# Broadcasting modulation rows and preparing the attention context inside the expert rounds of a one-core fp32 two-block transformer

## The reference, cut to what matters

```python
def second_block(x, c, ctx, c_ctx, w_mod, b_mod, norm_mix, ...):
    for i in range(2):                                  # i = 0: attention, i = 1: Fourier mixing
        sh1, sc1, g1, sh2, sc2, g2 = split(silu(c) @ w_mod[i] + b_mod[i], 6)
        h = rms_norm(x, norm_mix[i]) * (1 + sc1) + sh1
        if i == 0:
            csh1, csc1, *_ = split(silu(c_ctx) @ w_mod[i] + b_mod[i], 6)
            h_c = rms_norm(ctx, norm_mix[i]) * (1 + csc1) + csh1       # 256 context tokens
            y = gqa_attention(h, h_c, ...)              # keys and values of h and of h_c, queries of h
        else:
            y = fft2(h) @ w_o
        x = x + g1 * y
        x = x + g2 * hier_moe(rms_norm(x, norm_ffn[i]) * (1 + sc2) + sh2, ...)
    return rms_norm(x, final_norm)
```

## Time and profile before

| what | value |
|---|---|
| median of 3 runs | 2091.72 us |
| the profiled execution's own time | 2091.08 us |
| its span, first to last instruction | 2089.4 us |
| TensorE matmul busy | 1580.1 us (76%) |
| VectorE, ScalarE, GpSimd busy | 424.2, 258.0, 94.3 us |
| moved by DMA | 710.85 MB, 340 GB/s over the span |
| mean granted TensorE clock | 0.89 of 2.4 GHz |
| chain that ended last | DMA 47%, PE 40%, DVE 7%, ACT 2% |

### The profile page before, as it was taken

One profiled execution on the slowest core, in us unless ns is written; L12 is line 12 of the kernel. 1 busy time (PEld: TensorE's weight loads), 2 busy tenths in 40 slices (PEclk: granted clock), 3 DMA queues, 4 the chain that ended last, 5 costly groups with the idle time before them and its releaser, 6 DMA issues.

```text
span 2089.4 us, 22424 instructions
## 1 busy us (share of the span) xinstructions
PE 1580.1 (76%) x9852; PEld 730.5 (35%) x9852; DVE 424.2 (20%) x872; ACT 258.0 (12%) x539; POOL 94.3 (5%) x138
## 2 busy tenths in 40 slices
PE   8678877699878676899886766676687866676674
PEld 5445443384445343445432222222143322122221
DVE  0432111216431012365320000000034000000001
ACT  0220000025310001236100000000021000000000
POOL 1100000201100000020100000000000000000000
PEclk9799998799989999899998888888898988888887
DMA  9254999929959999059759999999944899999994
GB/s 376 70 221 203 423 424 423 360 97 385 370 191 423 423 424 414 19 202 372 298 218 424 424 423 423 423 424 424 422 182 186 351 423 423 423 424 424 423 424 203
DMA packets 122827, 710.85 MB, mean 340 GB/s; under 512 B 8408, under 2 KB 13448, under 8 KB 48992
## 3 DMA queue, kind: packets, MB, share of 16 engines
q1 hardware_dynamic: 116352, 697.14, 81.5%
q0 software_dynamic: 4272, 9.58, 1.5%
q10 hardware_dynamic: 2096, 2.57, 0.3%
HBM read 707.97 MB, written 1.05 MB: 339 GB/s over the span
## 4 chain that ended last, share of the span: by engine, by line
DMA 47%; PE 40%; DVE 7%; ACT 2%; SPq 1%; issue 1%; POOL 1%; ACTq 1%; DVEq 0%; POOLq 0%; PEldq 0%
DMA ring<-in_moe_w 22%; DMA work<-in_moe_w 10%; DMA ring<-in_moe_w_down 6%; DMA ring<-in_moe_w_up 5%; PE acc L1133 5%; PE pb L637 4%; PE pa L652 4%; DMA mod<-in_moe_w 3%; PE pb L624 3%; PE pa L670 2%; PE acc L917 2%; PE acc L711 2%; PE acc L1055 1%; PE acc L1900 1%; PE acc L1044 1%; SPq L580 1%
## 5 line engine op out<-in xcount | busy, mean ns | idle before, releaser
L637 PE MATMUL pb<-ring,XT 128*32 128x512 f32 x1440 | 275.1, 708 | 90.2 <-DMA ring<-in_moe_w 75.9
L652 PE MATMUL pa<-ring,work 128*32 128x512 f32 x928 | 195.2, 766 | 66.9 <-DMA ring<-in_moe_w 34.5
L637 PEld LDWEIGHTS pb<-ring,XT 128*32 128x32 f32 x1440 | 62.0, 125 | 247.4 <-DMA ring<-in_moe_w 115.5
L745 DVE TENSOR_TENSOR work<-work,pb 128x256 f32<-128x256 f32 (+1 forms) x32 | 17.7, 554 | 600.7 <-PE pb L637 456.7
L670 PE MATMUL pa<-work,HM 128*128 128x128 f32 x1024 | 130.3, 290 | 11.1 <-DVE work L733 11.1
L670 PEld LDWEIGHTS pa<-work,HM 128*128 128x128 f32 x1024 | 129.4, 206 | 24.9 <-issue 13.4
L711 PE MATMUL acc<-XT,work 128*128 128x512 f32 x256 | 118.4, 605 | 25.5 <-DVE XT L749 25.5
L637 PE MATMUL pb<-work,XT 128*32 128x512 f32 x448 | 102.4, 730 | 35.1 <-DMA work<-in_moe_w 35.1
L624 PE MATMUL pb<-ring,XT 128*32 128x256 f32 x1472 | 108.2, 391 | 26.4 <-DMA ring<-in_moe_w_up 17.4
L652 PE MATMUL pa<-work 128*32 128x512 f32 x448 | 90.2, 776 | 44.4 <-DMA work<-in_moe_w 27.1
L1133 PE MATMUL acc<-ring,XT 128*128 128x512 f32 x256 | 110.9, 594 | 2.7 <-ACT XT L1085 1.4
(11 more groups left out here) (392 smaller groups left out, 1706.9 us busy)
## 6 DMA issues: line engine op xcount, KB each, us to landing
ring<-in_moe_w SPq DMA_DIRECT2D x128, 2048.0 KB
work<-in_moe_w SPq DMA_DIRECT2D x44, 2048.0 KB
ring<-in_moe_w_up SPq DMA_DIRECT2D x24, 2048.0 KB
ring<-in_w_mod SPq DMA_DIRECT2D x48, 1024.0 KB
ring<-in_moe_w_gate SPq DMA_DIRECT2D x22, 2048.0 KB
ring<-in_moe_w_down SPq DMA_DIRECT2D x20, 2048.0 KB
mod<-in_moe_w SPq DMA_DIRECT2D x20, 2048.0 KB
work<-in_moe_w_down SPq DMA_DIRECT2D x12, 2048.0 KB
```

The lines of the kernel that those rows point to most:

```text
L637: last = nc.tensor.matmul(hbank[m][j * CAP:(j + 1) * CAP, :], m_xg[:, k, j * CAP:(j + 1) * CAP], slot_of(s0 + j // 2)[:, at:at + fn], star ...
L652: last = nc.tensor.matmul(pa[j * CAP:(j + 1) * CAP, h, :], m_ht[:, c, j * CAP:(j + 1) * CAP], slot_of(i)[:, at:at + 512], start=(c == 0), ...
```

## The change

The phases mod 0 and mod 1 are kept in the list but issue nothing. Their work is spread over the expert rounds:

- `rows_tensor` issues two row blocks in a round, after the gathered tokens are copied and ahead of the gate projection, into the two banks of `pa`; the stationary operand is one column of `select`, read with stride 0 over 128 columns. `rows_scalar` copies both blocks ahead of the silu. Rounds with row blocks: all 8 of moe 1 (first the context's four, then the token's twelve), rounds 1 to 5 of moe 2, and round 0 of moe 3 (the last two row blocks of layer 1, whose place is in use until the end of moe 2).
- `mod[:, 0:4096]` must be free of weights for that: `RETIRED` takes the three lent slots out of the ring in moe 1 after their first use (nine blocks, then a ring of six), and the one in `mod` in moe 2 (nine blocks, then a ring of eight).
- The context is loaded when round 0 of moe 1 has freed its six blocks. Its squares are taken in round 2, it is normed in round 3, multiplied and shifted by VectorE in rounds 4 and 5, and turned by TensorE in rounds 6 and 7, between the gate and the up projection (8 transposes into `pa`, copied by ScalarE).
- In gqa the keys and values of the context come first, as soon as moe 1 has ended on TensorE, and are copied by ScalarE; the squares of a token tile are taken as soon as its layer norm is done. The four row copies that stood ahead of them are gone.
- In fourier the squares start as soon as a tile is gated; the scale is made in round 3 of moe 2.

```diff
+RETIRED = {1: (6, 7, 8), 2: (8,)}
+MOD_ROWS = {1: {0: (12, 13), 1: (14, 15), **{g: (2 * g - 4, 2 * g - 3) for g in range(2, 8)}},
+            2: {g: (2 * g - 2, 2 * g - 1) for g in range(1, 6)}, 3: {0: (10, 11)}}
...
+        rest = [i for i in order if i not in RETIRED.get(ph.moe, ())] if ph.kind == "moe" else order
         for n in range(ph.slots()):
-            i = order[n % len(order)]
+            i = order[n] if n < len(order) else rest[(n - len(order)) % len(rest)]
...
                     last.then_inc(free[0], 2 * free[1])
+                    if m == 0:
+                        context_tensor(pe, ph, g)
...
             pe.wait_ge(r["xg_copied"], 2 * (t + 1) + START)
             if whole:
-                whole_up_tensor(pe, ph, wait_full, free, slot_of, hbank)
+                rows_tensor(pe, ph, g)
+                whole_up_tensor(pe, ph, g, wait_full, free, slot_of, hbank)
...
             pe.wait_ge(r["ht_copied"], t + 1 + START)
             if whole:
+                rows_done(pe, ph, g)
+                context_done(pe, ph, g)
                 whole_down_tensor(pe, ph, wait_full, free, slot_of)
...
             nc.scalar.copy(m_xg[:, 0:4, :], pa[:, 0, :].rearrange("p (k c) -> p k c", c=P)).then_inc(r["xg_copied"], 1)
+            if r is R[0]:
+                rows_scalar(act, ph, g)
             freed_gate(act)
             nc.scalar.activation(m_silu[:, 0:fn], pb[:, 0, 0:fn], ACT.Silu).then_inc(r["silu_done"], 1)
+            if r is R[0]:
+                context_scalar(act, ph, g)
...
+        def rows_tensor(pe, ph, g):
+            blocks = MOD_ROWS.get(ph.moe, {}).get(g, ())
...
             for i, n in enumerate(blocks):
-                if i == 0 or i == N_SHIFT_SCALE:
-                    pe.wait_ge(sel_ready, 2 * ph.layer + 1 + (i > 0))
-                if i >= 4:
-                    pe.wait_ge(row_copied, ph.rows0 + i - 3)
-                nc.tensor.matmul(mod_bank(i), d_sel[:, n, :], mod_rows[:, :], start=True, stop=True).then_inc(row_ps, 1)
-            pe.wait_ge(row_copied, ph.rows0 + len(blocks))
+                nc.tensor.matmul(pa[:, i, :], bc(select[:, n:n + 1], [P, P]), mod_rows[:, :], start=True, stop=True).then_inc(row_ps, 1)
...
+        def context_tensor(pe, ph, g):
+            if ph.moe == 1 and g >= ROUNDS - TT:
+                t = g - (ROUNDS - TT)
+                pe.wait_ge(cx_ready, 1)
+                rows_done(pe, ph, g)
+                for k in range(KC):
+                    last = nc.tensor.transpose(by_chunk(pa)[:, k, :], g_cx[:, t, k * P:(k + 1) * P], ident[:, :])
+                last.then_inc(cx_ps, 1)
...
         def gqa_tensor(pe, ph):
-            transpose_tensor(pe, HM, ph)
-            pe.wait_ge(xt_ready, 2 * (ph.xt + 1))
+            pe.wait_ge(R[0]["y_copied"], 2 * ROUNDS * 2 + START)
             for k in range(KC):
                 if k % 2 == 0:
                     slot_wait(pe, ph.slot0 + k // 2)
                 for t in range(TT):
+                    last = nc.tensor.matmul(pa[:, t, :], g_hct[:, k, t * P:(t + 1) * P], w_of(k)[:, D:D + 512],
+                                            start=(k == 0), stop=(k == KC - 1))
+            last.then_inc(kv_done, 1)
+            pe.wait_ge(cx_kv, 2 * TT)
+            transpose_tensor(pe, HM, ph)
+            pe.wait_ge(xt_ready, 2 * (ph.xt + 1))
+            for k in range(KC):
+                for t in range(TT):
                     last = nc.tensor.matmul(acc[:, 0, t * 512:(t + 1) * 512], XT[:, k, t * P:(t + 1) * P], w_of(k)[:, D:D + 512],
...
-            pe.wait_ge(cx_ready, 1)
-            transpose_tensor(pe, g_cx)
-            pe.wait_ge(xt_ready, 2 * (ph.xt + 2))
-            for k in range(KC):
-                for t in range(TT):
-                    last = nc.tensor.matmul(pa[:, t, :], g_hct[:, k, t * P:(t + 1) * P], w_of(k)[:, D:D + 512],
-                                            start=(k == 0), stop=(k == KC - 1))
-            last.then_inc(kv_done, 1)
...
         def gqa_scalar(act, ph):
+            for t in range(TT):
+                act.wait_ge(h_ready, TT * moe.lnh + t + 1)
+                square_scalar(act, X[:, t, :], 32 + t, flat_xt, tile_squares)
+            act.wait_ge(kv_done, 1)
+            for t in range(TT):
+                nc.scalar.copy(g_k[:, 2 + t, :, 0, :], pa[:, t, 0:256].rearrange("p (j e) -> p j e", j=NKV)).then_inc(cx_kv, 1)
+                nc.scalar.copy(g_v[:, 2 + t, :], pa[:, t, 256:512]).then_inc(cx_kv, 1)
             transpose_scalar(act, ph.xt, XT)
-            transpose_scalar(act, ph.xt + 1, g_hct)
...
         def ahead_pool(pool, ph):
             if plan[ph.i + 1].layer == 0:
-                pool.wait_ge(phase_done, ph.i)
-                pool.dma_start(ctx_in, a["ctx_2"][0].rearrange("(t p) d -> p t d", p=P)).then_inc(cx_loaded, 16)
+                pool.wait_ge(freed, ph.slot0 + 6)
+                pool.dma_start(g_cx, a["ctx_2"][0].rearrange("(t p) d -> p t d", p=P)).then_inc(cx_loaded, 16)
...
         def fourier_scalar(act, ph):
+            squares_scalar(act, ph.x0 - TT, flat_xt)
```

More of the change, by code:

```diff
@@ L79, in run_parts, with rows_before @@
     return [(w, 2 * pair, half), (w, 2 * pair + 1, half)]
+RETIRED = {1: (6, 7, 8), 2: (8,)}
+MOD_ROWS = {1: {0: (12, 13), 1: (14, 15), **{g: (2 * g - 4, 2 * g - 3) for g in range(2, 8)}},
+            2: {g: (2 * g - 2, 2 * g - 1) for g in range(1, 6)}, 3: {0: (10, 11)}}
+ROWS_BY = {"gqa": 16, "fourier": 26}
+def rows_before(moe, g):
+    return sum(len(ns) for m in MOD_ROWS for h, ns in MOD_ROWS[m].items() if (m, h) < (moe, g))
 class Place:
@@ new lines, in rows_tensor @@
+        def rows_tensor(pe, ph, g):
+            blocks = MOD_ROWS.get(ph.moe, {}).get(g, ())
+            if blocks:
+                layer = int(ph.moe > 1)
+                pe.wait_ge(bias_loaded, 16 * (layer + 1))
+                for n in (MODC - 2, MODC - 1):
+                    pe.wait_ge(rows_moved[n % 2], rows_count(layer, n))
+            for i, n in enumerate(blocks):
+                nc.tensor.matmul(pa[:, i, :], bc(select[:, n:n + 1], [P, P]), mod_rows[:, :], start=True, stop=True).then_inc(row_ps, 1)
@@ new lines, in rows_done, with rows_scalar @@
+        def rows_done(pe, ph, g):
+            if g in MOD_ROWS.get(ph.moe, {}):
+                pe.wait_ge(row_copied, rows_before(ph.moe, g) + 2)
+        def rows_scalar(act, ph, g):
+            blocks = MOD_ROWS.get(ph.moe, {}).get(g, ())
+            if (ph.moe, g) == (1, 2):
+                act.wait_ge(freed, ph.slot0 + 7)
+            if (ph.moe, g) == (1, 6):
+                act.wait_ge(cx_ready, 1)
+            if (ph.moe, g) == (2, 1):
+                act.wait_ge(freed, ph.slot0 + DEEP)
+            for i, n in enumerate(blocks):
+                act.wait_ge(row_ps, rows_before(ph.moe, g) + i + 1)
+                dst = mod[:, n * 512:(n + 1) * 512] if n < MODC else c_mod[:, (n - MODC) * 512:(n - MODC + 1) * 512]
+                nc.scalar.copy(dst, pa[:, i, :]).then_inc(row_copied, 1)
+            if (ph.moe, g) == (1, 2):
@@ L986, in weights_of, with context_scalar @@
+        def context_scalar(act, ph, g):
+            if ph.moe == 1 and g >= ROUNDS - TT:
+                t = g - (ROUNDS - TT)
+                act.wait_ge(cx_ps, t + 1)
+                nc.scalar.copy(g_hct[:, :, t * P:(t + 1) * P], by_chunk(pa)).then_inc(cx_copied, 1)
         def weights_of(w, cols, kk, i):
@@ L2156, in _ @@
                     router_vector(dve, ph, link)
-                    moe_other(dve, ph, lambda r, t, g, gate, up, every: round_vector(dve, ph, r, t, g, up, every), last=True)
-                    if ph.i + 1 < len(plan) and plan[ph.i + 1].kind == "mod":
-                        dve.sem_inc(work_free, 1)
+                    moe_other(dve, ph, lambda r, t, g, gate, up, every: round_vector(dve, ph, link, r, t, g, up, every), last=True)
                     if ph.fn == FN1:
@@ L2180, in make_plan @@
     slot = 0
-    moe = xt = h = ln = small = att = out_ = masked = rows = mix = x = 0
+    moe = xt = h = ln = small = att = out_ = masked = mix = x = 0
     for i, (kind, layer, fn) in enumerate(kinds):
@@ L2191, in make_plan @@
         ph.slot_mod = slot + {"nsa": 6, "gqa": 4}.get(kind, 0)
-        ph.rows0 = rows
-        rows += {0: 16, 1: 12}[layer] if kind == "mod" else 0
         ph.nout = {"ab": 5, "nsa": 8, "gqa": 8, "fourier": 2}.get(kind, 0)
```

143 lines of the change are left out of this document (71 added, 72 removed).

## The result

The changed kernel takes **2066.67 us** (median of 4 runs, 2064.21 to 2068.10), where the kernel before took 2091.17 in the same series (4 runs, 2090.08 to 2091.93): a ratio of 0.9882, 95% interval 0.9865 to 0.9899, 24.5 us less. Its profiled execution took 2068.10 us with a span of 2066.3.

A forecast was written before the change was run, and what follows sets the result against it. It took HBM to bound the expert phases and the engines' dependency chain the gaps between. Terms of -22.5, -3.3 and +1.8 summed to -24.0 us, giving a median of 2067.7 us, range 2061 to 2076.

The forecast's parts named there:

- Step 1: Moe 1 ends 5.4 us later, as block 13 waits for round 1's gate behind two rounds of rows; ends 4.3 to 8.8.
- Step 2: Layer norm to the tokens' keys: L1223 starts 5.4 us earlier, with the context's keys made beside the norm.
- the third rival: After moe 1, the context's keys are late (blocks late or TensorE cold), ending at 850: up to 5 us, 2072; chance 0.07.
- one of the two signs: Wrong if moe 1 ended over 10 us later, or TensorE still made the context's keys when the modulated tile was ready.
- Step 3: Behind L1223, the context's transposes, copy and L1232 leave the chain ahead of the keys' chain: -17.1 us.
- nothing is paid: L1223 stays warm between transposes (-2.1 us) and the DFT matmuls stay warm too (-2): 2063; chance 0.07.
- Step 4: Fourier stage after moe 2: input ready 5.3 us sooner, 2.0 lost to TensorE's clock after a pause: -3.3 us.
- Step 5: Moe 3, round 0: two row blocks ahead of the gate delay the first refill: +1.8 us, to 3.4.
- a starved ring: Moe 1, rounds 2 to 7: six slots starve DMA; at 5 us a round, 2097; chance 0.03.
- The worse start of moe 1: Row matmuls at 3.4 us, block 18 late, context displacing more: +10 to 12 instead of 5.4, 2073; chance 0.10.

The follow-up runs named there:

- no_load: The changed kernel with the context filled by a GpSimd memset instead of its 1 MiB load: 2067.59 us.
- ring_only: The kernel before with only the smaller rings (six slots in moe 1, eight in moe 2, after the first nine blocks): 2093.54 us.
- lent_no_load: The changed kernel with moe 1's own six slots taking blocks 0 to 5 and the context filled by GpSimd instead of loaded: 2066.48 us.
- own_first: The changed kernel with the context's key and value matmuls behind the tokens' own, as the kernel before had them: 2081.65 us.
- filler runs: Extra matmuls ahead of the Fourier stage: nine in the changed kernel, 2064.22 us; six in the changed kernel with late rows, 2059.35 us.
- all3: The changed kernel with late rows (moe 1 rounds 0 to 2, moe 3 round 0), own slots first in moe 1 and nine fillers: 2059.46 us.

## Why the prediction was right, point by point

**The total.** 2067.7 forecast, 2066.67 measured. The sum of the steps was -24.0; the spans differ by 23.1 and the medians by 24.5. The fit is better than the steps were. The profiled spans divide so: -22.0 up to the keys' chain, -1.3 from there to the end of moe 2, -2.6 in the DFT stage, +4.0 at the start of moe 3, -1.1 from its first refill to the end. The -1.3 and -1.1 stand in no step and their cause was not looked for; with them 2.4 us came that made up for the 2.9 by which steps 4 and 5 were too good. That part is luck. (The fast end of the range, 2091.7 - 29.3, is 2062.4, not 2062.0.)

**Step 1** (+5.4) came at +6.35, within its ends. Its mechanism is the one the runs show: block 13 waits for the gate of round 1, two rounds of rows lie ahead of that gate (1.93 and 1.90 us), and the load of the context is hidden (no_load). In the eight kernels whose block 13 waits for that gate, rows or none, gate 1 to last down is 179.2 to 179.9 us. What the ring adds without rows is 5.4 - 2 x 1.8 = 1.8 by the step, 2.4 by ring_only: 1.6 of it the wait of block 13, which the step had right, and 0.7 a term that it put at nothing, the stream at 421 instead of 424 GB/s from round 2 on. The rows were 1.9 each, not 1.8. The step had block 18 ready "just ahead" of need, with 1.3 us of slack; lent_no_load shows that this wait does bind when the one before is removed.

**Step 2** (L1298 5.4 us earlier) came at 2.76 + 0.49 = 3.25 early. With moe 1's end late by 0.95 more than forecast, 1.2 us remain. They are the context's keys, the third rival in small: the step gave TensorE VectorE's 1.7 us of branch, it took 3.86, and L1290 ran its first part at low clock (0.66 in 835 to 840), 15.68 us for 14.0. So it ended at 851.1 and not at 845.8, and the tile waited 1.4 us for its transposes. This is one of the two signs by which the prediction said it would be wrong: TensorE was still making the context's keys when the modulated tile was ready, if only by 0.2 us. The overlap of step 2 failed; it cost little.

**Step 3** (-17.1) held: own_first puts the context back and loses 15.0 us of the total. The group L1298 was 2.15 us faster than L1223, for TensorE now comes to it from work; the prediction had this only as part of the rival "nothing is paid". It repaid steps 1 and 2: the keys' chain starts 22.5 us earlier, the number of the forecast, by two misses that cancel, which is luck. Moe 2 kept the gain (its last down group comes 23.3 us earlier, 1481.84 for 1505.12): the rows in its rounds 1 to 5 cost nothing.

**Step 4** (-3.3 = -5.3 + 2.0): the tile came 5.2 us sooner, and the clock took back 2.5 (1.6 to 2.6 in the other kernels with this pause): net -2.6. The filler runs show the cause. The Trainium skill (TensorE: Matmul & The Clock Gate, What's actually happening) has the throttled clock as the default that activity lifts; the first eight at 6.22 us after 12 us without work, and at 3.60 to 3.70 behind fillers, agree.

**Step 5** (+1.8) came at +4.0 from issue to first refill. The rows' own term is right (1.98). The rest is what the step did not look at: the router's matmuls L502 take 6.37 us where L481 took 5.08, and the gather 6.66 for 6.20, 1.8 us together at the same tiles, and 0.3 of gaps. The trace shows the clock at work: in the first four microseconds of L502 the granted clock is 0.50, where L481 had 0.50, 0.50, 0.54 and 1.00; the tiles and what stands ahead of them are the same. They took 5.45 to 6.40 us in the nine other kernels that carry the change and keep its course, and 5.10 in ring_only, which doesn't, so it came with the change; how, was not tried.

The rivals: a starved ring came only as 0.7 us (421 GB/s from 650 on, for 423). The worse start of moe 1 did not come beyond 6.35. Late context keys came as 1.2 us. "Nothing is paid" held for L1298 alone.

## What to carry to other kernels

With a ring of slots, work placed ahead of a release delays every later transfer of the stage. The same work behind the release, where the engine waits for a moment anyway, cost 1.0 us a round here instead of 1.9, and nothing at the first release; with the rows of moe 3 moved too, the medians say 4.8 us in all. A transfer that is added beside a wait can cost nothing, and then taking it away gains nothing, as does taking away one of two waits when the other then holds the same stream. Where work is taken out of a pause, look at what the next matmuls lose in clock, and fill the pause to just short of its end: six fillers took 2.5 us off the stage, nine took 1.6 off or, in all3, made it longer. And where the gain sought is a microsecond or two, read the stage itself: medians and spans moved by as much in stretches that were the same.

## What the runs showed of the hardware that I had not expected

A selector column read with stride 0 as the stationary operand costs no more than a stored one: four instructions in 1.98 us, 592 ns each, with weight loads of 190 ns (L1290, with stored operands, has 592 and 190 as well). TensorE stands 3.7 to 4.5 us between its last expert matmul and the first instruction of the next stage even where the profile shows nothing awaited (L1290, and the fillers), VectorE 1.7 at the same place. And the granted clock falls to 0.50 also around short waits within a stage: behind waits of 1.6 to 3.8 us for DMA, the last down group of moe 1 took 5.08 to 6.45 us for the same 28 matmuls, according to where the clock came back, so that a gain of a microsecond ahead of it can be lost in it.
